# An encoder layer on eight cores: the first stage of the first sequence is set out by a planner, with scaling after the projections, and the memory norm moves into the attention

## The reference

```
h = RMSNorm(x)
u, q, k, v, gf, ga = split(h @ w_in)            # u: 256 wide; q, k, v: 3 groups of 256
A = real(fft2(u over positions, channels)) mixed per group
B = dilated window attention of the 3 groups (partial rotary on q, k), merged
x = x + (sigmoid(gf) * (A @ wf) + sigmoid(ga) * (B @ wa)) @ w_mix
x = x + CrossAttention(RMSNorm(x), RMSNorm(mem));  x = x + (relu(RMSNorm(x) @ w_up) ** 2) @ w_down
out = RMSNorm(x)
```

## Time and profile before

| | us |
|---|---|
| median of 4 runs | 2097.99 (2096.56 to 2099.67) |
| the profiled execution | 2099.67 |
| its span, first to last instruction, slowest core | 2097.7 |
| spans of the eight cores | 2089.2 to 2097.7 |
| first attention matmul of the first sequence, from the span's start | 135.40 |
| TensorE busy before it | 85.12 |

### The profile page before, as it was taken

How to read it: one execution, slowest core, us unless ns; L and a number is a source line. 1 busy time by engine, 2 the same in 40 slices (tenths; PEclk the granted TensorE clock), 3 DMA queues, 4 the chain that set the end, 5 groups by cost and what they waited for, 6 DMA issues and landing times.

```text
span 2097.7 us, 30871 instructions; the slowest of 8 cores (2089.2 to 2097.7 us)
## 1 busy us (share of the span) xinstructions
PE 1983.2 (95%) x10282; PEld 973.8 (46%) x10282; DVE 981.6 (47%) x1586; ACT 771.0 (37%) x1309; POOL 418.6 (20%) x391
## 2 busy tenths in 40 slices
PE   4779979999999999999999997999999999999996
PEld 2445534455444444444445663445544444444443
DVE  4554662355454333334875467225645433333354
ACT  4444552246542143212434555224654211111243
POOL 2200013353240033100340001325314000000033
PEclk9999999999999999999999999999999999999998
DMA  8532326066110244223455222606610022222112
GB/s 199 134 76 61 53 49 181 1 121 114 28 43 19 43 121 117 43 61 77 140 145 143 61 41 41 201 1 109 117 37 1 1 40 41 41 41 41 21 71 91
DMA packets 40523, 155.42 MB, mean 74 GB/s; under 512 B 4785, under 2 KB 19250, under 8 KB 30130
## 3 DMA queue, kind: packets, MB, share of 16 engines
q0 software_dynamic: 11808, 75.50, 20.5%
q1 hardware_dynamic: 28128, 77.61, 11.8%
q10 hardware_dynamic: 434, 0.35, 0.1%
HBM read 205.87 MB, written 16.78 MB: 106 GB/s over the span
## 4 chain that ended last, share of the span: by engine, by line
PE 85%; DVE 5%; ACT 3%; issue 3%; DMA 2%; POOL 1%; SPq 1%; DVEq 0%; ACTq 0%; POOLq 0%
PE ps L147 85%; DVE arena L147 5%; ACT arena L147 3%; DMA arena<-arena 1%; POOL arena L147 1%; DMA arena<-x 1%; SPq L145 0%; ACT L147 0%; DVEq L141 0%; ACTq L141 0%; SPq L147 0%; POOLq L141 0%; SPq L141 0%
## 5 line engine op out<-in xcount | busy, mean ns | idle before, releaser
L147 PE MATMUL ps<-arena 128*128 128x512 bf16 (+4 forms) x10282 | 1983.2, 355 | 106.4 <-ACT arena L147 59.5
L147 PEld LDWEIGHTS ps<-arena 128*128 128x128 bf16 (+1 forms) x10282 | 973.8, 100 | 1115.5 <-issue 188.6
L147 ACT ACTIVATE arena<-ps 128x512 bf16<-128x512 f32 (+4 forms) x812 | 489.1, 624 | 970.5 <-PE ps L147 801.6
L147 DVE TENSOR_TENSOR arena<-arena 128x512 bf16<-128x512 bf16 (+8 forms) x607 | 310.4, 531 | 605.4 <-ACT arena L147 586.6
L147 POOL TENSOR_TENSOR arena<-arena 128x512 f32<-128x512 f32 (+2 forms) x299 | 364.4, 1220 | 770.2 <-ACT arena L147 518.2
L147 DVE TENSOR_TENSOR arena<-ps,arena 128x512 f32<-128x512 f32 (+3 forms) x376 | 294.1, 790 | 244.9 <-PE ps L147 243.6
L147 ACT ACTIVATE arena<-arena 128x512 f32<-128x512 f32 (+3 forms) x451 | 261.3, 589 | 320.9 <-DVE arena L147 214.9
L147 DVE SCALAR_TENSOR_TENSOR arena<-arena 128x512 bf16<-128x512 f32 (+3 forms) x328 | 218.1, 708 | 51.8 <-ACT arena L147 51.3
L147 POOL DMA_DIRECT2D arena<-wb x62 | 33.6, 544 | 676.9 <-PE ps L147 635.6
L147 DVE SCALAR_TENSOR_TENSOR arena<-arena,ps 128x512 f32<-128x512 f32 x128 | 82.0, 684 | 151.3 <-PE ps L147 146.5
L147 DVE SCALAR_TENSOR_TENSOR arena<-ps,arena 128x512 f32<-128x512 f32 x64 | 43.5, 687 | 32.5 <-PE ps L147 32.5
(11 more groups left out here) (3 smaller groups left out, 0.3 us busy)
## 6 DMA issues: line engine op xcount, KB each, us to landing
arena<-wb POOLq DMA_DIRECT2D x62, 1024.0 KB, 9.8
arena<-x SPq DMA_DIRECT2D x40, 512.0 KB, 3.9
arena<-x SPq DMA_DIRECT2D x8, 2048.0 KB, 14.1
out<-arena SPq DMA_DIRECT2D x28, 512.0 KB, 2.6
arena<-wa POOLq DMA_DIRECT2D x20, 512.0 KB, 9.7
arena<-rope SPq DMA_DIRECT2D x6, 1024.0 KB, 10.7
arena<-arena SPq DMA_DIRECT2D x96, 64.0 KB, 2.3
arena<-x SPq DMA_DIRECT2D x16, 256.0 KB, 11.4
```

The costliest lines, as they stand in the source:

```text
L147: ins = getattr(eo, o['name'])(*o['args'], **o['kw'])
```

## The change

For the first sequence the hand-written order is replaced by `first_stage`, which describes the stage as jobs (engine, guessed duration, due number, what it needs, and the earliest time by a table of arrival times) and records them in the order in which a list scheduler, `run_jobs`, would start them.

- x comes in 32 DMAs of one chunk each (before: 24, of two chunks each, the first 16 over 256 positions), the first weights in halves.
- For tiles 0 and 1 the matmuls don't wait for the norm: `conv` writes x times the gain into `hT` (ACT and DVE in turn), the units run on that, and the output is multiplied by the root as it leaves PSUM (`unit_out`, by DVE; for v by ACT with a scale per position from `columns` and `column_root`). Later `apply` overwrites those parts of `hT` with the normed values; that of tile 0 (`last_apply`) stands behind the Fourier transform.
- For tiles 2 and 3 the norm comes first, as before, at full width.
- The sum over the partitions is one f32 matmul instead of two bf16 ones; twelve matmuls on zeros run at the start.
- Four of the v units, the gathers, the folds and the rotation are jobs among the others.
- The memory norm (`mem_gen`) is loaded behind the rotation and stepped along the filler of `attn(0)` and `attn(1)`.
- Both sequences: the Fourier matrices come in two halves and, in the second sequence, are asked for after tile 1 and not after tile 3; several buffers move; `proj_gen` takes the tiles from 3 down to 0.

```diff
-            if b_ == 0:
-                load_xin(0, 0, 0, 256)
-                aload(0)
-                load_consts()
...
-                norm1_sq(0, 0, ns=0, t0=0, n=256, eng=0)
-                norm1_fin(0, 0, 0, 0, 256)
...
+            def run_jobs(jobs):
+                end, free, left = {}, {}, dict(jobs)
+                while left:
+                    best = None
+                    for name, (eng, dur, due, f, deps, ready) in left.items():
+                        if all(d in end for d in deps):
+                            t = max([ready, free.get(eng, 0.0)] + [end[d] + (0.15 if jobs[d][0] != eng else 0.0) for d in deps])
+                            if best is None or (t, due) < best[:2]:
+                                best = (t, due, name)
...
+                def load_x(tg, c, after=()):
+                    return dma('sp', xin[tg][:, c, :], dr['x'][0, tg].rearrange("p (c t) -> p c t", c=8)[:, c, :], 'x%d%d' % (tg, c), after)
...
+                def conv(tg, c):
+                    g_ = gains[:, 0, c:c + 1]
+                    if c % 2:
+                        OP('dve', 'tensor_scalar', hx(tg, c), xin[tg][:, c, :], g_, None, ALU.mult, reads=[xin[tg][:, c, :], g_], writes=[hx(tg, c)])
+                    else:
+                        act(hx(tg, c), xin[tg][:, c, :], AF.Copy, scale=g_)
...
+                def sums(tg):
+                    mm(psf(7), ones32, part[tg % 2][0], True, True)
...
+                    if tg >= RAW:
+                        act(dst, src, AF.Copy)
+                    else:
+                        tt('dve', dst, src, r1[tg], ALU.mult)
...
+                ARR = [[t + d * c for c in range(8)] for t, d in ((6.5, 1.6), (21.0, 1.0), (29.0, 1.1), (38.5, 1.0))]
+                WH = [(8.1, 12.5, 16.3), (18.5, 20.0, 21.5)]
...
+                run_jobs(jobs)
+                for i in range(4, 8):
+                    aload(i, gs if i > 5 else ())
+                return lambda: [apply(0, c) for c in range(8)]
...
+            for j in range(2):
+                for odd in range(2):
+                    dft_unit(j, odd, ALLB)
+            dft_mid(ALLB)
+            if b_ == 0:
+                last_apply()
             v_ones(1)
...
-                    which, c, tg = n // 8, (n // 4) % 2, n % 4
+                    which, c, tg = n // 8, (n // 4) % 2, 3 - n % 4
...
+            interleave(attn(0), with_mem(proj_gen(1)), lambda k: 1 if k % 4 != 3 else 0)
```

More of the change, by code:

```diff
@@ L546, in v_ones, with folds @@
                 OP('pool', 'memset', o_, 1.0, writes=[o_])
-            def folds():
-                for j in range(2):
+            def folds(j):
+                if True:
                     u = uT[:, j, :]
@@ L603, in load_dft @@
             def load_dft():
[L604 to L608, removed]
-                for k in range(8):
[L610 to L614, removed]
+                src = dr['dft'].rearrange("p (i k n t) -> p i k n t", i=2, k=2, n=4)
@@ new lines, in load_dft, with mem_gen @@
+                for i in (1, 0):
+                    dma('sp', dfth[i], src[:, i], 'dft%d' % i)
+            def mem_gen():
+                dma('sp', memst, dr['mem'][b_].rearrange("p (c m) -> p c m", c=8), 'mem')
+                for _ in range(4):
+                    yield
+                acc_, hi, lo = ssacc[:, 0:256], nset[0][1][0][:, 0:256], nset[0][1][1][:, 0:256]
+                for k in range(8):
+                    act(sqm[k % 2] if k else acc_, memst[:, k, :], AF.Square)
+                    yield
+                    if k:
+                        tt('pool', acc_, acc_, sqm[k % 2], ALU.add)
+                yield
+                act(hi, acc_, AF.Copy)
+                yield
+                tt('dve', lo, acc_, hi, ALU.subtract)
+                yield
+                o = psf(P.bank(FB))[:, 0:256]
+                mm(o, ones, hi, True, False)
+                mm(o, ones, lo, False, True)
+                yield
+                act(rstd[:, 0:256], o, AF.Ln, scale=1.0 / D, bias=eps)
+                act(rstd[:, 0:256], rstd[:, 0:256], AF.Exp, scale=-0.5)
+                yield
+                for c in range(8):
+                    stt(memn[:, c, :], memst[:, c, :], gains[:, 2, c:c + 1], rstd[:, 0:256], ALU.mult, ALU.mult)
+                    yield
@@ new lines, in run_jobs @@
+            def run_jobs(jobs):
[7 more added lines that the diff above has]
+                                best = (t, due, name)
+                    t, _, name = best
+                    eng, dur, _, f, _, _ = left.pop(name)
+                    free[eng] = end[name] = t + dur
+                    f()
@@ L616, in build_program @@
             QK = ((0, 0), (0, 1), (1, 0), (1, 1))
             if b_ == 0:
[L618 to L640, removed]
@@ L650, in build_program @@
                         popp(i, 0, 2 if tg else 0)
[L651 to L657, removed]
+                    if tg == 1:
+                        load_dft()
+                gather(0, 0)
+                gather(0, 1)
+                for j in range(2):
+                    folds(j)
+                drain(rotate(0))
+                for i in range(8):
+                    v_unit(0, 2 * i, ALLB)
             zx_unit()
@@ L808, in proj_gen, with with_mem @@
                     yield
-            for j in range(2):
-                for odd in range(2):
-                    dft_unit(j, odd, ALLB)
-            dft_mid(ALLB)
-            interleave(attn(0), proj_gen(1), lambda k: 1 if k % 4 != 3 else 0)
+            mg = mem_gen() if b_ == 0 else iter(())
+            def with_mem(gen):
+                for _ in gen:
+                    next(mg, None)
+                    yield
+            interleave(attn(0), with_mem(proj_gen(1)), lambda k: 1 if k % 4 != 3 else 0)
             v_ones(2)
-            interleave(attn(1), proj_gen(2), lambda k: 1 if k % 4 != 3 else 0)
+            interleave(attn(1), with_mem(proj_gen(2)), lambda k: 1 if k % 4 != 3 else 0)
             merged = view(M0, 16384, pat="p (g c t) -> p g c t", g=4, c=8)
```

224 lines of the change are left out of this document (160 added, 64 removed).

## The result

The changed kernel is faster, but by 7.7 us less than forecast. Against the kernel before, run on the same chip in turn, its time has the ratio 0.9845 (95% interval 0.9810 to 0.9879). In some executions the cores of one die ran at a lower granted clock: the times given here leave those executions out, the ratios only those that were slowed by more than about 1.5%, and where a traced execution has such cores (nowait, wbf) the mean of the other die's four stands in brackets. Six executions of the changed kernel took 2063.94 to 2066.60 us, their median is 2064.7, and the profiled one took 2064.12 (span 2063.1, core 6), 35.5 less than that of before. Forecast were 2057 and a range of 2046 to 2076.

A forecast was written before the change was run, and what follows sets the result against it. TensorE's work in the first stage was taken as the bound. First attention matmul at 91.5 not 135.40 us saves 43.9, less 3.0 given back is 40.9: 2099.67 to 2058.8, median 1.7 lower, 2057 us; range 2046 to 2076.

The forecast's parts named there:

- What bounds, and where: First sequence's stage before attention: its floor is TensorE's work, busy for only 85.12 of 135.40 us.
- The loading: Start of first stage: 10.05 MB up to chunk 4 of tile 3, at 204 then 248 GB/s, landing at 44.1 us.
- the rival with the chunks one behind the other: First-stage x loads: smaller loads halve the early rate to 102 GB/s, chunk 4 of tile 3 lands at 76; 2089 us, chance 0.05.
- TensorE's catching up: First stage, tiles 0 and 1: matmuls left from about 18.5 us, v units and two f32 sums end near 42.5.
- the hole of 4.7 us: TensorE before tile 2: idle some 4.7 us, from near 42.5 until tile 2 starts at 47.2.
- the path that I named: Before tile 2: chunk 4 of tile 3 lands at 44.1, square and root follow, first apply at 46.3, TensorE at 47.2.
- From tile 2 to the attention: TensorE from 47.2: tiles 2 and 3, z and Fourier units to 89.5; first attention matmul at 91.5 us.
- the sign I had named for a wrong forecast: First stage on DVE: folds still running at 85 us would show the forecast wrong.
- the rotary path: End of first stage: DVE done at 83.5, issues 2.0, landing 5.25, so rotary rows at 90.7 us (87.8 to 96.0).
- Given back: Attention after the first stage: 0.5 us for last_apply ahead of masks, 2.5 for the moved memory norm, 3.0 together.
- The landing that bites: Rotary transfer takes 10.48 us again (+5.2) and the memory norm costs 8.5 (+6): 2068 us, chance 0.15.
- The low clock: TensorE fed by chunks, 18 to 75 us: 11 windows at 0.66 lose 19 us, less the one counted; 2075 us, chance 0.10.

The follow-up runs named there:

- nowait: Changed kernel with tile 1's first x chunk asked for at once, not after chunk 6 of tile 0; 2067.06 and 2068.35 us, ratio 0.987.
- wbf: Changed kernel with the six first weight pieces read from a bf16 tensor of other numbers, without a cast; 2059.85 and 2060.70 us, ratio 0.984.
- memonly: Kernel before with only its memory norm moved, stepped along the filler of attn(0) and attn(1); median 2088.97 us, ratio 0.9955.
- nowarm: Changed kernel without the twelve matmuls on zeros at the start; median 2064.35 us, ratio 0.9837.
- wfirst: Changed kernel with all six first weight pieces asked for at the start, none behind a chunk of x; median 2068.92 us, ratio 0.9859.

## Why the prediction was right in kind and 7.7 us short

**What bounds, and where: right.** The floor was read as TensorE's work in the first stage, and from 29.98 us on the stage runs near it (5.2 us idle of 69.9).

**The loading: the term that was mis-sized.** Chunk 4 of tile 3 landed at 49.4 in the mean (49.09 on core 6) and not at 44.1. The queue view of core 6 up to that landing (q1 is x, q0 the weights, 31.5% of 49.09 us and so on):

```profile
q1 hardware_dynamic: 4511, 8.38, 62.0%
q0 software_dynamic: 1008, 2.10, 31.5%
```

Set against the forecast's own terms, each at its 248 GB/s, in us of all 16 engines (the first 20 us at 204 GB/s moved what takes 16.4 at 248, so 3.6 of them count as the slow start):

| | forecast | core 6 |
|---|---|---|
| four weight pieces, 2.10 MB as written | 8.5 | 15.5 |
| x up to that chunk, 7.60 MB | 30.6 | 27.6 (3.63 a MB) |
| x behind that chunk, moved before it had landed, 0.78 MB | 0 | 2.8 |
| constants, 0.35 MB | 1.4 | 1.4 |
| slow start (forecast), queues empty (measured) | 3.6 | 1.7 |
| lands at | 44.1 | 49.0 |

The weights were 7.0 us too cheap; x and the start were too dear by 4.9; and 2.8 us were left out: a transfer is split over the 16 engines, the parts of chunk 4 landed from 45.8 to 49.1, and engines that were done with theirs had gone on to the chunks behind. wbf takes the cast away and lands that chunk at 44.2, so that 44.1 is met only without the cast. The rates of the earlier trace rows that I used were averages over both kinds of load.

The rule of the Trainium skill weighed there ("DMA: Bandwidth & Descriptors", section "Bandwidth": batch to a MiB or more) would have had the small chunks pay; the first 20 us had a queue share of 0.89 with loads of 256 KB, so the rival with the chunks one behind the other fell. The fit used in the prediction is one for loads that GpSimd issues, while x is issued by SyncE.

**TensorE's catching up: size right in part by luck, start wrong.** I counted some 24 us of work for tiles 0 and 1 from about 18.5 on, ending at 42.5. It took 25.25 us, but from 29.98, since tile 1's first chunk landed at 28.45 and the last of the six weight pieces at 27.98. I had let all of it lie there at 18.5, though x of tile 1 stood behind tile 0 and the weights in the same sum. That the size fits is partly luck: some 37 of the 96 matmuls, not 27, lay before 29.98 (2.2 us less), and this was made up by the 16 products of `columns` (2.1 us), which I had left out, and by a window at 0.66 (1.7), which I had put behind the hole.

So the hole of 4.7 us shrank to 1.68, and tile 2 started at 56.90 and not 47.2 (9.7 later). What held it was this backlog, and not the landing of chunk 4, as I had it. ACT on core 6:

```profile
52.77 1.03 ACT L147 ACTIVATE arena<-ps,arena 128x256 bf16<-128x256 f32 x2
53.70 0.62 ACT L147 ACTIVATE arena<-arena 128x512 f32<-128x512 f32 x1
```

The second row is the square of chunk 4. It starts 4.6 us after the landing (49.09), behind copies of v units, which wait for TensorE; on all eight cores it starts 2.0 to 7.2 us after it. So the path that I named, from that landing by the square and the root to tile 2, set the start of tile 2 on no core.

Even with that chunk landing as forecast (wbf, 44.2) the attention starts at 94.56 and not 91.5: there PE still has tiles 0 and 1 until 49.6 (core 0 of wbf, first attention 94.31):

```profile
23.67 25.94 PE L147 MATMUL ps<-arena 128*128 128x512 f32 x153 [1.02 <-DVE arena L147]
51.30 1.24 PE L147 MATMUL ps<-arena 128*128 128x512 bf16 x5 [1.69 <-DVE arena L147]
```

About 5 us of the miss is thus the loading's size, by a run. The other 3 or so is what is left; it fits this start, but no run shows it by itself.

**From tile 2 to the attention: right, by 1.3 us.** 56.90 to 99.91 is 43.0; forecast 44.3. The z units end at 88.57 (31.7 us behind tile 2's start, forecast 31.9), the Fourier units take 9.6 for 8.7. DVE, at the same time:

```profile
74.08 3.23 DVE L147 TENSOR_TENSOR arena<-arena 128x1023 f32<-128x1023 f32 x4 [0.24 <-ACT arena L147]
...
86.69 2.28 DVE L147 STREAM_SHUFFLE arena<-arena 128x2048 bf16<-128x2048 bf16 x1
89.14 3.69 DVE L147 TENSOR_TENSOR arena<-arena 128x2048 bf16<-128x2048 bf16 x3 [0.17 <-DVE arena L147]
...
98.12 1.54 DVE L147 TENSOR_TENSOR arena<-ps,arena 128x512 bf16<-128x512 f32 x2 [0.28 <-PE ps L147]
99.55 5.38 DVE L147 SCALAR_TENSOR_TENSOR arena<-arena 128x512 bf16<-128x512 f32 x8
```

The folds run until 86, the sign I had named for a wrong forecast, shifted with tile 2. The last product ends at 92.83, and the eight issues behind it:

```profile
92.95 5.64 SPq L145 DMA_DIRECT2D arena<-arena  x8
```

They landed 3.3 us after issue (median). The first four had landed by 98.75 on core 6, 0.9 us ahead of the end of the Fourier sums at 99.66, and on all eight cores the first attention matmul waits for DVE. So the path by TensorE came last, by a little; the forecast had the rotary path later (90.7 against 89.5), with a landing of 5.25 us. On some cores of other runs (1 and 5 of nowait, 4 of wbf) the wait reads `<-DMA arena<-arena`. The conversion on DVE, taken at 0.67, took 0.617; the f32 sum, taken at 0.9, shows two records of 0.62 mean in sequence, 1.1 a pair.

**Given back: 1.3 us, not 3.0.** The term of 2.5 for the memory norm was too large: memonly gives 0.2. What is left of the 1.3 in the mean is not told apart from `last_apply` (forecast 0.5) and the spread of cores (1959.7 to 1963.2).

**The rivals.** The landing that bites (2068) is near the measured time for another reason: the transfer took 3.3 us and the memory norm nothing. The low clock: after 20 us core 6 has one window under 1.00, 30 to 35 at 0.66: as many as counted, but in the work of tile 1 and not behind the hole. Cores 0 and 4 have two, at 0.50 to 0.58, and are the two whose attention starts last (101.69 and 101.81), 1.8 us behind core 6. The rule of the Trainium skill named there ("TensorE: Matmul & The Clock Gate", section "What's actually happening") agrees with that row, which follows the sparse work from 20 to 30. SyncE's issues took 0.67 us at the median and the last began at 39.2:

```profile
L147 SPq DMA_DIRECT2D arena<-x x32: 328/672/1732, 1.1 to 39.2; - x32
```

**Where 35.0 us came from.** The memory norm's place: 10.2, put into the kernel before. Scaling behind the matmuls: 12.4, taken out of the changed kernel. If these add up, which no run shows, 12.4 are left for the rest (norms at full width, the v units, folds and rotation as jobs of the planner; all eight v units are such jobs).

## What to carry to other kernels

Where a stage is held up by loading, take the rate of each kind of load from a stretch in which only that kind fills the queues: here a casting load took about what its read bytes would take. A chunk counts as landed with its last part, so count what the other engines move meanwhile. Then put each consumer's start at the landing of its own data, not at the end of the consumer before it. An earlier landing is worth only what the next wait leaves of it: ask for which chunk ends the stage before moving others ahead of it.

## What the runs showed that was not expected

Twelve warm-up matmuls bought nothing. On core 6 four matmuls behind them took 1.02 us; on the other seven cores the first matmuls on data come at 12.0 to 12.7 us and take 0.43 us each, as without a warm-up. The window from 10 to 15 us is at 0.50 to 0.55 on all eight cores, when TensorE has little to do. Core 6:

```profile
5.00:10.00 5.00, 3.11 (x10) 0.76 (x7) 0.48 (x1) 3.43 (x6) 0.00 (x0) 1.00 1.01 184
10.00:15.00 5.00, 2.48 (x6) 0.79 (x7) 1.18 (x2) 1.69 (x3) 1.66 (x4) 0.53 1.02 196
```

Without them (nowarm, core 1) the clock column reads 1.00 where the first six matmuls take 2.72 us, 0.45 each:

```profile
10.00:15.00 5.00, 2.74 (x7) 0.80 (x7) 1.18 (x2) 1.87 (x3) 0.22 (x1) 1.00 1.06 273
```

In wfirst six matmuls of the same form take the same 2.72 us (core 1) in a window that reads 0.53. The first clock record of a core in nowarm's trace comes at 14.2 to 20.3 us, at 15.6 on core 1; ahead of it the column reads 1.00 whatever the clock. On core 6 that lasts until 20.3, while matmuls take 0.43 us each until 20.0. So the column can't be trusted ahead of the first record; the duration of a matmul can.
